# Weights laid out by unit, the router's rounding moved ahead, and an end in halves, in a two-model transformer kernel

## The chip, the core and the metric

The kernel runs on one core of a Trainium2 chip. The metric is the device time of one execution in microseconds (us); the time before is the median of three runs. Five engines work at once: TensorE (PE, matrix products, with PEld for the loads of its stationary operand), VectorE (DVE), ScalarE (ACT), GpSimd (POOL) and SyncE (SP). They meet by semaphores. DMA engines move data between the memory off the core and the on-chip memory of 128 partitions; products land in PSUM, eight banks of 512 fp32 numbers per partition.

## The reference

One sequence of 256 tokens, width 1024, goes through two models of two layers each, all in fp32. All weights are used once or, in the experts' stage, once per round.

```python
for l in range(2):                      # first model
    mod = silu(c) @ w_ada[l] + b_ada[l] # six vectors: shifts, scales, gates
    proj = modulate(rmsnorm(x, norm1_g[l]), shift1, scale1) @ w_in[l]
    # three attentions (latent, stick-breaking, block), gated, merged
    x = x + gate1 * (merged @ w_out[l])
    h = modulate(rmsnorm(x, norm2_g[l]), shift2, scale2)
    x = x + gate2 * (square(relu(h @ w_ff1[l])) @ w_ff2[l])
x = rmsnorm(x, final_norm_g)
x = layer_norm(a * x + retention(x), ...)        # second model, layer 0
x = layer_norm(a * x + swiglu(x, ffn_w_in, ffn_w_out), ...)
x = layer_norm(a * x + sparse_attention(x), ...) # layer 1
logits = x @ w_router                            # 8 experts, the best 2 per token
gate = softmax over the best 2
x = layer_norm(a * x + sum_e gate_e * swiglu(x, moe_w_in[e], moe_w_out[e]), ...)
```

## The kernel before

**Products.** An fp32 product is made of three products of rounded parts: `hi*whi + lo*whi + hi*wlo`. Weights come in units of 512 KB, [128 partitions, 2 blocks, 512 columns]. For each unit SP issues one load into a ring of buffers (`raw`, 4 deep; 12 deep in the experts' stage, over `raw`, `mod_b`, `work` and `spare`), ACT rounds it into `whi` (L1386), DVE subtracts into `wlo` (L1969), and PE runs the products: `unit` (L466 with whi, L472 with wlo) or, where the next stage wants tile 0 early, `by_tile` with `half_unit` (L486, L491). `pass_units(n)` is the place in the programs of ACT and DVE where n units are split, three units ahead of PE (`LEAD`). Activations are turned (transposed) on PE against an identity (L519, L566, L577) and split into `xh`, `xl` or `yh`, `yl` by ACT and DVE (L1440, L1447, L2052, L2059).

**Loads.** The weights lie in memory as the reference has them. `rows` (L3221) picks 256 rows and 512 columns as [p, 2, 512], so each partition gets two runs of 2 KB. SP issues them in the order of use, in loops for the dense SwiGLU and the experts. `load` (L3168) waits until the buffer's former unit has been split. Modulation weights (`w_ada`) go through the one buffer `ada_raw` or, in between, through `raw`; DVE sums them by L1990 and L1993, and `mod_used` lets SP load the next.

**Start.** 16 units of `w_ada` are loaded into idle buffers (`first_raw`, L3324), with x (1 MB) after the eighth; PE and DVE sum them, DVE scales and shifts x, and the first projection follows.

**From the sparse stage to the experts.** The last chunk of the sparse stage runs by tile (`last_chunk`, L1226). DVE's `layer_norm_by_tile` (L2560) adds the columns (L2538), takes moments (L2542), asks ACT for the root (L1532) and scales (L2554, L2557); it turns tile 0 and splits units in between. Then `experts` starts: PE turns both tiles of x (`turn_tiles`, L558), waits for one more hand-over from DVE (L1232), and runs the router's 24 products (L1238). That hand-over comes after ACT has rounded the router (L1861), DVE has taken its remainder (L2922), ACT has rounded x into `xth` (L1863) and DVE has made `xtl` (L2926). The logits are turned, DVE finds the best two (L2932 to L2950), ACT takes the exponential (L1867), PE counts places (L1250 to L1254), DVE forms the gates and the number of rounds, scales x by ALPHA (L2971), and all engines read the number of rounds. SP holds back all expert loads but the first three until then.

**Experts' loop.** For each of eight experts the tokens that chose it are gathered by products with a one-hot matrix (L1266), 128 at most in a round. An expert has seven steps; each step has eight units of the way in (`step_in`), the turn of the hidden part, and four of the way out (`step_out`). At an expert's end ACT rounds the output (L1875, 128 x 1024), DVE takes the remainder (L2993), PE scatters it by the one-hot's transpose (L1285, L1286) in four pieces, and DVE adds them to x (L3003). These pieces are woven into the next expert's units. The loop over experts runs two experts a pass.

**End.** After the last expert there is no next unit to hide these steps. DVE takes the moments of both tiles (L2515), ACT both roots (L1923), DVE scales tile by tile (L2527, L2530), and one store of 1 MB (L3350) writes x.

## Time and profile before

| What | us |
|---|---|
| Median of three runs | 2870.45 (2865.42 to 2870.57) |
| Profiled execution, its time | 2874.83 |
| Profiled execution, its span | 2872.9 |
| PE busy | 2683.1 |
| DVE busy | 2114.7 |
| ACT busy | 1610.5 |
| Mean granted clock of PE | 0.962 of full speed |
| Data moved | 666.09 MB |

A view of the profile is read as follows. A row of a timeline has start, duration, engine, line of the kernel, operation, what is written from what, and in brackets the idle time of the engine before it and who ended that. A row of the waits has the engine and line that waited, the one that released it, and the total, the number and the longest. The chain is followed back from the last instruction, at each step to what released it. PEclk is the clock granted to PE: 1.00 is 2.4 GHz, 0.50 is 1.2 GHz. Durations of PE's products overlap, so their pace is read from the chain or from starts.

### The profile page before, as it was taken

The numbers are of one execution on the slowest core, as the hardware profiler recorded it, in microseconds if no ns is written. First come the engines' busy times: TensorE is split into PE (matmuls) and PEld (weight loads), VectorE is DVE, ScalarE is ACT, GpSimd is POOL, SyncE is SP. The second block draws the span as 40 slices with busy tenths as digits, with TensorE's granted clock in tenths as the row PEclk, the third lists the DMA queues.
The fourth block names the chain that finished last, engine by engine and source line by source line (L and its number), as shares of the span: only waits on it lengthen the run. The fifth ranks groups of instructions, "written<-read, shape, count | busy, mean of one in ns | idle before, by whom it ended". The sixth has DMA issues, their size and how long they took to land.

```text
span 2872.9 us, 39552 instructions
## 1 busy us (share of the span) xinstructions
PE 2683.1 (93%) x12874; PEld 2166.5 (75%) x12874; DVE 2114.7 (74%) x2488; ACT 1610.5 (56%) x2094; POOL 21.5 (1%) x39
## 2 busy tenths in 40 slices
PE   7899999988999999999999887899999999999997
PEld 5677778876777787777997765688878878888875
DVE  6765577677556755866556855699989988999998
ACT  3544444445544444444444543577767777777775
POOL 0000000000000000000000000000000000000000
PEclk8999999999999999999999978899999999999998
DMA  8655468755545655645655411799989999999995
GB/s 300 196 156 166 154 199 266 242 183 170 169 147 164 204 188 155 219 150 153 194 181 166 137 44 44 262 353 329 365 300 364 330 342 334 345 347 331 366 358 199
DMA packets 358114, 666.09 MB, mean 232 GB/s; under 512 B 23024, under 2 KB 57456, under 8 KB 357344
## 3 DMA queue, kind: packets, MB, share of 16 engines
q1 hardware_dynamic: 354080, 647.66, 67.3%
q0 software_dynamic: 3904, 16.76, 1.8%
q8 instruction: 73, 1.20, 0.2%
q14 instruction: 57, 0.47, 0.0%
HBM read 663.29 MB, written 1.05 MB: 231 GB/s over the span
## 4 chain that ended last, share of the span: by engine, by line
PE 81%; DVE 8%; ACT 4%; issue 2%; DVEq 2%; DMA 1%; SPq 0%; ACTq 0%
PE ps L466 44%; PE ps L472 22%; PE ps L486 2%; DVE wlo L1969 2%; PE ps L577 2%; ACT whi L1386 1%; PE ps L491 1%; PE ps L1266 1%; PE ps L676 1%; DVE mod_sum L1993 1%; DMA ada_raw<-in_w_ada 1%; PE ps L788 1%; DMA proj<-in_w_ada 1%; PE ps L646 0%; ACT att L1608 0%
## 5 line engine op out<-in xcount | busy, mean ns | idle before, releaser
L1969 DVE TENSOR_TENSOR wlo<-raw,whi 128x1024 fp32r<-128x1024 f32 x709 | 863.4, 1224 | 452.9 <-ACT whi L1386 441.1
L1386 ACT ACTIVATE whi<-raw 128x1024 fp32r<-128x1024 f32 x709 | 746.0, 1059 | 703.1 <-PE ps L472 615.1
L466 PE MATMUL ps<-whi,xh 128*128 128x512 f32 (+3 forms) x1248 | 457.3, 377 | 4.5 <-ACT proj L1426 4.0
L466 PE MATMUL ps<-whi,xl 128*128 128x512 f32 (+3 forms) x1248 | 443.5, 366 | 0.0
L466 PE MATMUL ps<-whi,gathered_hi 128*128 128x512 f32 x896 | 362.8, 405 | 9.7 <-ACT whi L1386 6.3
L466 PE MATMUL ps<-whi,gathered_lo 128*128 128x512 f32 x896 | 356.1, 397 | 0.0
L472 PE MATMUL ps<-wlo,xh 128*128 128x512 f32 (+3 forms) x1248 | 293.5, 362 | 0.0
L472 PE MATMUL ps<-wlo,gathered_hi 128*128 128x512 f32 x896 | 283.3, 397 | 0.2 <-DVE wlo L1969 0.2
L466 PEld LDWEIGHTS ps<-whi,xh 128*128 128x128 f32 x1248 | 240.4, 193 | 46.1 <-ACT proj L1426 4.8
L466 PEld LDWEIGHTS ps<-whi,xl 128*128 128x128 f32 x1248 | 240.5, 193 | 36.9 <-issue 2.2
L472 PEld LDWEIGHTS ps<-wlo,xh 128*128 128x128 f32 x1248 | 215.8, 191 | 38.4
L466 PE MATMUL ps<-whi,yh 128*128 128x512 f32 (+2 forms) x592 | 236.8, 402 | 4.4 <-DVE yl L2059 2.2
L466 PE MATMUL ps<-whi,yl 128*128 128x512 f32 (+2 forms) x592 | 229.1, 389 | 0.0
L1969 DVE TENSOR_TENSOR wlo<-spare,whi 128x1024 fp32r<-128x1024 f32 x168 | 204.5, 1224 | 19.0 <-ACT whi L1386 17.4
L1969 DVE TENSOR_TENSOR wlo<-mod_b,whi 128x1024 fp32r<-128x1024 f32 x168 | 205.5, 1223 | 17.7 <-ACT whi L1386 12.6
L1386 ACT ACTIVATE whi<-spare 128x1024 fp32r<-128x1024 f32 x168 | 179.0, 1065 | 52.0 <-PE ps L472 52.0
L1386 ACT ACTIVATE whi<-mod_b 128x1024 fp32r<-128x1024 f32 x168 | 178.3, 1061 | 52.5 <-PE ps L472 52.1
L466 PEld LDWEIGHTS ps<-whi,gathered_hi 128*128 128x128 f32 x896 | 169.6, 189 | 48.5 <-ACT whi L1386 7.2
L472 PEld LDWEIGHTS ps<-wlo,gathered_hi 128*128 128x128 f32 x896 | 169.3, 189 | 41.9 <-DVE wlo L1969 0.7
L466 PEld LDWEIGHTS ps<-whi,gathered_lo 128*128 128x128 f32 x896 | 169.8, 189 | 37.1
L466 PE MATMUL ps<-whi,hidden_hi 128*128 128x512 f32 x448 | 178.5, 398 | 2.3 <-DVE hidden_lo L2059 1.3
L466 PE MATMUL ps<-whi,hidden_lo 128*128 128x512 f32 x448 | 176.9, 395 | 0.0
(417 smaller groups left out, 3587.2 us busy)
## 6 DMA issues: line engine op xcount, KB each, us to landing
raw<-in_moe_w_in SPq DMA_DIRECT2D x227, 512.0 KB, 5.4
spare<-in_moe_w_in SPq DMA_DIRECT2D x165, 512.0 KB, 5.6
mod_b<-in_moe_w_out SPq DMA_DIRECT2D x165, 512.0 KB, 5.4
raw<-in_w_ff SPq DMA_DIRECT2D x128, 512.0 KB, 4.6
raw<-in_w_in SPq DMA_DIRECT2D x96, 512.0 KB, 3.7
work<-in_moe_w_in SPq DMA_DIRECT2D x56, 512.0 KB, 5.5
work<-in_moe_w_out SPq DMA_DIRECT2D x56, 512.0 KB, 5.2
ada_raw<-in_w_ada SPq DMA_DIRECT2D x48, 512.0 KB, 4.5
```

Source lines behind the costliest of these rows:

```text
L466: e.matmul(ps[0:lhs[2], banks[t], at:at + width], part[:, k0 + j, t * P:t * P + lhs[2]], whi[:, slot, w], start=first and j == 0 and part ...
L472: mm = e.matmul(ps[0:lhs[2], banks[t], at:at + width], lhs[0][:, k0 + j, t * P:t * P + lhs[2]], wlo[:, slot, w], start=False, stop=last an ...
L486: e.matmul(ps[:, bank, at:at + width], part[:, k0 + j, t * P:(t + 1) * P], whi[:, slot, w], start=first and j == 0 and part is lhs[0], sto ...
L491: mm = e.matmul(ps[:, bank, at:at + width], lhs[0][:, k0 + j, t * P:(t + 1) * P], wlo[:, slot, w], start=False, stop=last and j == blocks - 1)
L577: tr = e.transpose(ps[:, bank, (j * tiles + t) * P:(j * tiles + t + 1) * P], src(t, b + j), ident)
L676: mm = e.matmul(ps[:, 4 + t, h * HD:(h + 1) * HD], side_pT[g][:, at:at + P], v(b, h), start=b == 0, stop=b == t)
L788: mm = e.matmul(ps[:, 4 + t, (h0 + h) * HD:(h0 + h + 1) * HD], own_pT[i % 2][:, w], proj[:, b, at:at + HD], start=b == 0, stop=b == t)
L1266: mm = e.matmul(ps[:, bank, j * P:(j + 1) * P], part[:, t, k * P:(k + 1) * P], onehot[b][:, t, :], start=t == 0, stop=t == 1)
L1386: e.activation(whi[:, slot, :], src, ACT.Copy).then_inc(split_hi, 1)
L1969: e.tensor_tensor(wlo[:, slot, :], src, whi[:, slot, :].bitcast(F32), ALU.subtract).then_inc(split_lo, 1)
L1993: last = e.scalar_tensor_tensor(total, w[:, j, :], c_col[:, k:k + 1], total, ALU.mult, ALU.add)
```

## The change

Four parts, in one version.

1. **Layout.** Weights other than the narrow part of `w_in`, `w_uq`, the `cmp` weights and the gates of the sparse stage are rearranged before the launch (`in_tiles`), so that each unit of 512 KB lies in one piece, 4 KB for each partition; `tile` takes the place of `rows` in the loads. `ffn_w_in` is laid out in four blocks of 256 columns. The narrow part of `w_in` and the gates become arrays of their own. The number of loads and their order stay.
2. **Router.** The router is rounded at unit 30 and its remainder taken at unit 31 of the sparse stage. `layer_norm_ahead_of_experts` takes the place of `layer_norm_by_tile` there: no units are split in it, and tile 1's columns are added before tile 0 is turned. PE's router products no longer wait for `xth` and `xtl`. Three splits, `xtl` and the scaling by ALPHA stand at new places of DVE's program. PE runs 14, 4 and 8 products on zeros (`idle`) after the turn of tile 0, after the logits' turns and after the place products. ACT runs one small Exp and one small Silu ahead of their use.
3. **Rounding of an expert's output** in two halves of 512 columns on ACT and DVE; the scatter goes by halves first and then by tiles, and its bank goes by tile.
4. **End.** Moments and roots by tile; the last scaling and the store in pieces: tile 0 whole, tile 1 in two halves.

```diff
+IDLE = (14, 4, 8)
...
             def experts(e):
-                turn_tiles(e, lambda t, b: x[:, t, b * P:(b + 1) * P], KB)
+                def idle(n):
+                    for _ in range(n):
+                        e.matmul(ps[:, 5, :], zero[0:1, 0:P], zero[0:1, :], start=True, stop=True)
+                tile_turns(src, 0)(e)
+                idle(IDLE[0])
+                tile_turns(src, 1)(e)
                 turned(e)
                 clear(e)
-                source(e)
...
+                idle(IDLE[1])
                 source(e)
...
+                idle(IDLE[2])
                 source(e)
...
-                    return [part(t, n) for t in range(NT) for n in range(2)]
+                    return [part(t, n) for n in range(2) for t in range(NT)]
...
             def experts(e):
                 turn_second(e)
-                vec(e)
-                e.activation(router_h, router, ACT.Copy).then_inc(act_ready, 1)
-                vec(e)
                 e.activation(xth, x[:, :, :], ACT.Copy).then_inc(act_ready, 1)
+                e.activation(st[:, 30:31], k_("eps"), ACT.Exp)
...
-                    e.activation(eh, ps[:, 2:4, :].rearrange("p b n -> p (b n)"), ACT.Copy).then_inc(out_hi, 1)
+                    for n in range(2):
+                        e.activation(eh[:, n * 512:(n + 1) * 512], ps[:, 2 + n, :], ACT.Copy).then_inc(out_hi, 1)
...
                 def one_round(e, r):
+                    e.activation(st[:, 30:31], k_("eps"), ACT.Silu)
...
+            def layer_norm_ahead_of_experts(e, units, src):
+                pass_units(e, 1)
+                take_gain(e, 0)
+                take_gain(e, 1)
+                tile_done(e)
+                add_columns(e, 0, 1, src(0, 1))
+                tile_deviation(e, 0)
+                normed_tile(e, 0)
+                e.wait_ge(unit_used, c.at("unit", RING + units - 1))
+                add_columns(e, 1, 1, src(1, 1))
+                tile_deviation(e, 1)
+                turn_first(e)
+                normed_tile(e, 1)
...
             def experts(e):
+                pass_units(e, 1)
                 turn_second(e)
-                e.wait_ge(extra_small, 80)
-                to_act(e)
-                from_act(e)
-                e.tensor_tensor(router_l, router, router_h.bitcast(F32), ALU.subtract)
-                e.drain()
-                to_act(e)
+                pass_units(e, 1)
                 from_act(e)
                 e.tensor_tensor(xtl, x[:, :, :], xth.bitcast(F32), ALU.subtract)
-                to_pe(e)
+                e.drain()
+                e.tensor_scalar(x[:, :, :], x[:, :, :], ALPHA, None, ALU.mult)
...
                 to_act(e)
+                pass_units(e, 1)
                 from_act(e)
...
-                e.tensor_scalar(x[:, :, :], x[:, :, :], ALPHA, None, ALU.mult)
...
+            def tile(w, column, group, groups=4):
+                return w[bass.ds((column * groups + group) * P, P), :]
...
+            rows_out = out.rearrange("o (t p) n -> p (o t) n", p=P)
             sp.wait_ge(x_done, 1)
-            sp.dma_start(out.rearrange("o (t p) n -> p (o t) n", p=P), x[:, :, :]).then_inc(stored, 16)
-            sp.wait_ge(stored, 16)
+            sp.dma_start(rows_out[:, 0, :], x[:, 0, :]).then_inc(stored, 16)
+            for h in range(2):
+                sp.wait_ge(x_done, 2 + h)
+                sp.dma_start(rows_out[:, 1, h * 512:(h + 1) * 512], x[:, 1, h * 512:(h + 1) * 512]).then_inc(stored, 16)
+            sp.wait_ge(stored, 48)
...
+def in_tiles(w, blocks=UROWS):
+    *lead, rows, columns = w.shape
+    wide = D // blocks
+    w = w.reshape(*lead, rows // (blocks * P), blocks, P, columns // wide, wide)
+    k = len(lead)
+    w = w.transpose(*range(k), k + 3, k, k + 2, k + 1, k + 4)
+    return w.reshape(*lead, -1, D)
```

## Rows read from the trace of the kernel before

**Rows 1.** The page: busy time by engine, PE first, share of the span, instructions

```profile
PE 2683.1 (93%) x12874; PEld 2166.5 (75%) x12874; DVE 2114.7 (74%) x2488; ACT 1610.5 (56%) x2094; POOL 21.5 (1%) x39
```

**Rows 2.** Windows: PE, PEld, DVE, ACT, POOL busy; PEclk; DMA share; GB/s

```profile
46.00:1765.00 1719.00, 1598.91 (x8095) 1306.32 (x8095) 1118.56 (x1419) 799.40 (x1183) 14.69 (x24) 0.96 0.55 172
...
1870.00:2840.00 970.00, 962.50 (x4313) 773.41 (x4312) 873.63 (x882) 740.00 (x825) 0.00 (x0) 0.99 0.97 344
```

**Rows 3.** Waits, 1870 to 2840 us: total, times, longest

```profile
ACT whi L1386 <- PE ps L472: 161.3, 418, 1.2
...
PE ps L466 <- ACT whi L1386: 6.3, 2, 3.8
```

**Rows 4.** Waits of the load queue (SP), 1870 to 2840 us

```profile
SPq L3218 <- DVE wlo L1969: 510.3, 627, 7.8
```

**Rows 5.** Windows of the start, columns as in rows 2

```profile
5.00:10.00 5.00, 2.75 (x4) 1.23 (x5) 3.67 (x18) 0.28 (x1) 0.00 (x0) 1.00 1.03 363
15.00:20.00 5.00, 1.98 (x4) 0.68 (x4) 0.89 (x2) 0.00 (x0) 0.00 (x0) 1.00 1.01 411
```

**Rows 6.** Chain that ended last, 0 to 46 us: start, us, what

```profile
9.19 16.30 DMA proj<-in_w_ada
```

**Rows 7.** The same chain, 46 to 120 us

```profile
56.10 4.68 DMA ada_raw<-in_w_ada
```

**Rows 8.** The same chain, 1776 to 1832 us

```profile
1776.05 0.46 PE ps L491 x2
...
1778.90 0.59 DVE x L2538
...
1780.95 1.23 DVE wlo L1969
...
1784.89 1.98 PE ps L566 x8
...
1790.87 2.29 DVE yl L2926
1793.45 4.29 PE ps L1238 x24
...
1809.71 7.07 PE ps L1266 x32
...
1818.67 2.07 PE ps L466 x4
...
1824.00 0.93 PE ps L466 x4
```

**Rows 9.** Timeline of DVE, 1798 to 1809 us; in brackets idle time before

```profile
1798.48 0.17 DVE L2074 COPY att<-ps 128x8 f32<-128x8 f32 x1 [5.31 <-PE ps L1245]
...
1805.64 1.20 DVE L2971 TENSOR_SCALAR x<-x 128x2048 f32<-128x2048 f32 x1
```

**Rows 10.** Timeline of ACT, 1832 us

```profile
1832.12 1.28 ACT L1627 ACT_TABLE_LOAD   x1
```

**Rows 11.** Window of the first gather, columns as in rows 2

```profile
1809.70:1818.60 8.90, 7.76 (x34) 7.19 (x34) 1.71 (x4) 1.83 (x4) 0.00 (x0) 0.50 1.02 387
```

**Rows 12.** Timeline of DVE at the end

```profile
2852.66 1.23 DVE L2993 TENSOR_TENSOR out_lo<-ps,out_hi 128x1024 fp32r<-128x1024 f32 x1
...
2859.09 2.65 DVE L2515 BATCH_NORM_STATS2 st<-x 128x6 f32<-128x512 f32 x4 [0.30 <-issue]
...
2866.99 1.28 DVE L2530 SCALAR_TENSOR_TENSOR x<-x,st,gain_b 128x1024 f32<-128x1024 f32 x1
```

**Rows 13.** Waits, 2090 to 2100 us

```profile
ACT out_hi L1875 <- issue: 6.3, 1, 6.3
...
PE ps L466 <- ACT whi L1386: 3.8, 1, 3.8
```

**Rows 14.** DMA issues of the whole run: xcount, KB each, us to landing

```profile
raw<-in_w_uq SPq DMA_DIRECT2D x6, 256.0 KB, 2.7
...
out<-x SPq DMA_DIRECT2D x1, 1024.0 KB, 3.9
```

More of the change, by code:

```diff
@@ L1279, in piece @@
                         def piece(e):
[L1280 removed]
+                            if t == 0:
                                 c.add("out")
@@ L1817, in sigmoids, with router_rounded @@
                     return e.activation(nsa_gate[:, 1, :], ps[:, b + 1, 0:48], ACT.Sigmoid)
+                def router_rounded(e):
+                    e.wait_ge(extra_small, 80)
+                    e.activation(router_h, router, ACT.Copy).then_inc(act_ready, 1)
                 at(4, twice_values)
@@ L1921, in act_program @@
             experts(act)
-            act.wait_ge(vec_ready_last, 1)
-            act.activation(st[:, 8:10], st[:, 0:2], ACT.Sqrt).then_inc(last_root, 1)
+            for t in range(NT):
+                act.wait_ge(vec_ready_last, t + 1)
+                act.activation(st[:, 8 + t:9 + t], st[:, t:t + 1], ACT.Sqrt).then_inc(last_root, 1)
         def gather_pieces(jobs, copies):
@@ L2990, in output @@
                 def output(e):
[L2991 to L2994 removed]
+                    for n in range(2):
+                        w = slice(n * 512, (n + 1) * 512)
+                        c.add("out")
+                        e.wait_ge(out_hi, c.at("out"))
+                        e.tensor_tensor(el[:, w], ps[:, 2 + n, :], eh[:, w].bitcast(F32), ALU.subtract).then_inc(out_lo, 1)
                 def add_output(b):
@@ L3196, in ada_rows @@
                 l, _, _, first = MOD_CHUNKS[m // 4]
-                return rows(a["w_ada"][l], m % 4 * UROWS * P)[:, :, first:first + 512]
+                return tile(a["w_ada"][l], first // 512, m % 4)
             def load_own_modulation(e, m):
@@ L3223, in rows, with columns, tiled @@
                 return w[bass.ds(at, blocks * P), :].rearrange("(j p) n -> p j n", p=P)
-            def columns(e, w, n_rows, first, width=UCOLS):
+            def tile(w, column, group, groups=4):
+                return w[bass.ds((column * groups + group) * P, P), :]
+            def columns(e, w, n_rows, first, width):
                 for i in range(units_of(n_rows)):
                     load(e, rows(w, i * UROWS * P)[:, :, bass.ds(first, width)])
-            def mlp_in(e, w_in, width, kind, s, units=range(8), first=False):
-                wide = kind[0]
+            def tiled(e, w, n_rows, column):
+                for i in range(units_of(n_rows)):
+                    load(e, tile(w, column, i, units_of(n_rows)))
@@ L3232, in mlp_in @@
+            def mlp_in(e, w_in, steps, kind, s, units=range(8), first=False):
                 for u in units:
                     if kind is SWIGLU and u < 4:
-                        load(e, rows(w_in, u % 2 * 512, 4)[:, :, bass.ds(s * wide + u // 2 * width, wide)])
+                        load(e, tile(w_in, s + u // 2 * steps, u % 2, 2))
                     elif kind is EXPERT:
-                        load_expert(e, rows(w_in, u % 4 * 256)[:, :, bass.ds(s * wide + u // 4 * width, wide)], first)
+                        load_expert(e, tile(w_in, s + u // 4 * steps, u % 4), first)
@@ L3237, in mlp_in, with mlp_out @@
                     elif u < 4:
-                        load(e, rows(w_in, u % 4 * 256)[:, :, bass.ds(s * wide + u // 4 * width, wide)])
-            def mlp_out(e, w_out, kind, s, by_columns=False):
-                order = [(kg, n) for kg in range(kind[0] // 256) for n in range(2)]
+                        load(e, tile(w_in, s, u % 4))
+            def mlp_out(e, w_out, steps, kind, s, by_columns=False):
+                groups = kind[0] // 256
+                order = [(kg, n) for kg in range(groups) for n in range(2)]
@@ L3285, in layer @@
                             for k in range(2):
-                                load(e, rows(a["w_out"][l], (2 * half + k) * UROWS * P)[:, :, n * 512:(n + 1) * 512])
+                                load(e, tile(a["w_out"][l], n, 2 * half + k))
             def experts(e):
```

169 lines of the change are left out of this document (84 added, 85 removed).

## The prediction

> **What bounds the kernel now.** I read the page first: TensorE (PE) is busy 93% of the span, and the chain that ended last is mostly PE [rows 1]. Then the stages. The experts' stage, 1870 to 2840 us, is a third of the span: PE is busy 962.5 of 970 us, while the DMA engines are busy 0.97 of it at 344 GB/s [rows 2]. Two resources look full, so the waits have to say which is late. ScalarE (ACT), which rounds each weight unit, waits for PE 418 times (161.3 us), and no wait for a DMA is in that list; PE waits for ACT twice [rows 3]. The load queue itself waits for VectorE (DVE) to free a buffer, 627 times, 510.3 us [rows 4]. So loads run ahead of need and the stage is PE's. Its pace in the chain is 0.93 us for four products with whi and 0.46 us for two with wlo, 1.40 us a unit [rows 8].
>
> That leaves the places where PE stands still or runs at 1.2 GHz: the start, where loads are late [rows 5, 6]; the modulation loads of the two attention layers [rows 7]; the way from the sparse stage's last layer norm to the first expert unit, 1776 to 1824 us [rows 8 to 11]; two stops inside the experts' loop [rows 13]; and the end [rows 12].
>
> **The change part by part.** The sum is against the profiled execution: 2874.83 us (span 2872.9), which lies 4.4 us above the 2870.45 us median. I carry differences over to the median.
>
> *Layout of the weights.* Each unit's 512 KB becomes 4 KB a partition in one run instead of two of 2 KB. The number of loads, their order and waits are unchanged; only their speed can change. In the experts' stage a faster load brings nothing: the queue waits for buffers anyway. If that cover were gone, PE would wait for units. At the start loads are on the path: the load of proj ends 16.30 us after its issue [rows 6], and DVE's first sums hang on it at 25.5 us. The rate was 363 GB/s in 5 to 10 us and 411 in 15 to 20 us, when x (rows of 4 KB) was among the loads [rows 5]. So 4 KB runs are worth between 0 and 13%. I take 5%, nearer to the low end since x was only a part of that traffic and the engines were full in both rows: over about 20 saturated us that is 0.9 us (0 to 2). From 25.5 to 42 us the start hangs on DVE, which is untouched.
> The trace reaches 411 GB/s from HBM with one core busy. The Trainium skill ("DMA: Bandwidth & Descriptors", Where 436 GB/s comes from) says the HBM side binds at about 358 GB/s; by it 4 KB runs would bring nothing here, 2853.3 us in all. The row speaks against that cap. The same page (Why small descriptors are slow) gives some 3 cycles a packet beside 32 bytes a cycle; my estimate from it is 134 against 131 cycles for 4 KB, 2%, or 0.4 us.
> The modulation's chunks that use ada_raw have one buffer: load, two DVE sums, next load. Four of these loads are in the chain, 4.5 to 6.8 us each; one stands for them [rows 7]. 5% of some 21 us, less where a fixed latency stays, is 0.8 us (0 to 1.6).
>
> *Layer norm before the experts.* Before, DVE turned tile 0 (two subtractions of about 0.69) before it added tile 1's columns at 1778.9, and it put a wlo split of 1.23 us (1780.95) ahead of tile 1's scaling [rows 8]. PE had ended the products at 1776.5, so the add can start at 1776.6. The chain from there to tile 1's turn was 6.0 us; it loses the split (1.2) and gains the two subtractions (1.3) in the shadow of ACT's root. The turn moves from 1784.89 to 1782.7: **2.2 us**.
> *Router.* Between the turn (1784.89) and the router's products (1793.45) lie 8.56 us [rows 8]: the turn, router_hi on ACT, router_lo on DVE, then xth on ACT and xtl on DVE (2.29), since the products waited for all of it. The rounding moves to units 30 and 31 of the sparse stage (ACT 0.26 us and DVE 0.22 us there; from 46 to 1765 us ACT is busy 799 and DVE 1119 of 1719 us [rows 2], so I cost it at nothing; without that cover it would cost those 0.5 us). The products then need only the turn's parts: 3.3 us after the turn's start, at 1785.5 to 1786.0. xtl, one split (1.23) and the ALPHA scaling (1.20) now run on DVE beside the products: 1785.3 + 1.2 + 2.3 + 1.2 with a wait for xth gives 1790.3. The products (4.29 us at mixed clock) end at 1788.4 to 1790.3, so DVE's copy of the logits, 1798.48 before [rows 9], goes to 1790.3. What is late next is this scaling on DVE, not PE. **8.2 us** so far, the first 2.2 included.
> *After it.* The scaling (1.20 at 1805.64) no longer stands before the rounds' value [rows 9]; a short wait for ACT's copy (0.4) falls away. The split placed after the exponential's hand-over delays DVE by 1.2 us, but the place products on PE (about 3.2 us) end later than DVE's chain then does. Together **9.7 us** by the first gather (1809.71 before). Reading the value stays. SP's remaining first loads start with it, 9.7 us earlier, as before.
>
> *Idle products.* 14, 4 and 8 products on zeros stand in PE's gaps. At 2.4 GHz they take about 0.23 us each (3.3, 0.9, 1.9 us), and the gaps are 5.3, 3.8 and 2.5 us, so they cost nothing; at 1.2 GHz the last 8 take 3.7 us and would put the gather 0.3 to 1 us later. What they can bring: before, the gather was PE-busy 7.76 us at a granted clock of 0.50 [rows 11], which is 1.2 GHz, after a gap of 6.6 us (1786.87 to 1793.45) and shorter ones; it took 7.07 us, and the two units after it 5.33 us (1818.67 to 1824.00) for 2.8 warm [rows 8]. At 2.4 GHz the gather is 3.5 us: 6.0 us at most. The trace before has no idle products in a gap, so 0 and 6 are the ends. A granted clock of 0.99 on average held through PE's short waits in the experts' stage [rows 2], which lies on the side of 6; gaps of 1.6 to 2.9 us remain around the idle products, which lies on the side of 0. I take **4 us**.
> The Trainium skill ("TensorE: Matmul & The Clock Gate", Part 1) has a clock that is released by activity, and Part 4 says that turns in PE mode do not count as such; the idle products are ordinary ones, so by it they would count and the turns between them not. No row here shows either.
> *Silu's table.* 1.28 us of table load stood between PE's last product of the first chunk and the activation [rows 10]. Loaded ahead, the activation starts when PE ends (1832.4 for 1833.41): **1.0 us**.
> *Rounding in halves.* Inside the loop ACT and DVE each do 0.2 us more per expert, under PE. The scatter's new order of banks leaves the same number of products.
>
> *End.* The first half's remainder is ready 0.95 us sooner (half of DVE's 1.23 [rows 12] and of ACT's rounding, which is a little shorter, less some 0.2 for the fixed part of an instruction), and DVE's adds shift by that. Then the statistics by tile cost 4.0 us for 3.8 (2859.09 to the first scaling) [rows 12], the reciprocals and four halves for two whole passes 0.5 more: DVE ends 0.2 us sooner. The last store is 256 KB, not 1 MB: landing 3.9 us for 1 MB, 2.7 for 256 KB [rows 14], which is 1.2, and 1.9 by rate. Sum **1.7 us** (1 to 3).
>
> Sum: 0.9 + 0.8 + 9.7 + 4.0 + 1.0 + 1.7 = **18.1 us**. 2874.8 becomes 2856.7, and the median 2870.45 becomes **2852.4 us**.
>
> **Rivals.**
> (A) The clock is not held: PE turns tile 1 and runs the router's products cold (1.0 us more on the way), and the idle products give nothing. For it: PE fell cold in every gap of this stretch, and gaps remain. 18.1 - 4 - 1 = 13 us, **2857**.
> (B) The experts' stops change. Twice PE stood 3.8 and 2.5 us while ACT had nothing it waited for but "issue", at the loop's way back [rows 13]; with the cold clock after it about 5 us each. They fall together with full DMA queues, so shorter loads may shorten them, and a longer loop body may add one. Both gone: 18 + 10, **2842**. One more: 2857.
> (C) Slower: the new layout lowers the rate. A unit of 512 KB per 1.40 us is 374 GB/s at PE's pace, and the stage had 344 GB/s at a DMA share of 0.97 [rows 2], so there is no reserve. The price begins where the rate of contiguous units falls below 344: at 330 GB/s the stage's 334 MB take 1011 us for 970, **2893**. Against it: the highest rates of the trace came with 4 KB rows.
> (D) The gain does not reach the path: another wait (the exponential, the place products, SP's first units) takes the gather's place, and the stage ends within 5 us of before, **2867**.
>
> **How the numbers follow.** Forecast 0.55, A 0.24, B 0.08, C 0.06, D 0.07. The range from 2841 (B, or clock 6, start 2, end 3) to 2863 (A with none of the load terms, a shorter end gain and one longer stop) leaves out C, D and the tails. A measurement of this kernel tells about 0.2%, 5.7 us, from no change: C is slower; most of D is the same. Faster 0.88, same 0.06, slower 0.06.
>
> **What would show it.** Router products starting about 8 us after the last product of the sparse stage (17 before); a gather of 3.5 us at a granted clock of 1.00 if the idle products work, 7 us at 0.50 if A; DVE idle before its logit copy gone; no table load before the first Silu; in 5 to 35 us the same DMA share with some 5% more GB/s; the experts' stage at 344 GB/s still with no DMA in ACT's waits; the last store landing in some 2.5 us. The prediction is wrong if ACT starts to wait for units, or if the stops at the loop's way back multiply.

## The result and the profile after

Five runs of the changed kernel have a median of **2853.98 us** (2852.68 to 2857.76), five of the kernel before one of 2870.57 us. The ratio is **0.9949**, 95% interval 0.9938 to 0.9961: 0.5% faster, 16.6 us between the medians. The forecast was 2852.4 us, so the total came out as forecast, and in part by luck: two of its parts did not, and they cancelled. The profiled execution of the kernel after took 2853.45 us, that of before 2874.83, so the two traces differ by more than the medians: 21.2 us of span. The page of the kernel after, answering to [rows 1]:

```profile
span 2851.7 us, 39687 instructions
...
PE 2683.9 (94%) x12900; PEld 2165.7 (76%) x12900; DVE 2114.5 (74%) x2501; ACT 1609.8 (56%) x2105; POOL 21.5 (1%) x39
...
PEclk9999999999999999999999978899999999999999
```

Nothing of the work is gone: PE is busy 2683.9 us for 2683.1 (26 products on zeros are new). What went is time in which it stood still or ran at 1.2 GHz. The windows of the kernel after (columns as in [rows 2]), for the start [rows 5], the experts' stage [rows 2] and the first gather [rows 11]:

```profile
5.00:10.00 5.00, 3.58 (x5) 1.55 (x6) 3.76 (x17) 0.28 (x1) 0.00 (x0) 1.00 1.02 409
...
15.00:20.00 5.00, 2.66 (x6) 0.68 (x4) 1.50 (x2) 0.00 (x0) 0.00 (x0) 1.00 1.00 416
1855.00:2825.00 970.00, 965.29 (x4340) 775.00 (x4339) 879.85 (x894) 744.45 (x836) 0.00 (x0) 1.00 0.94 344
1799.30:1807.50 8.20, 7.75 (x35) 7.21 (x34) 1.68 (x3) 1.19 (x2) 0.00 (x0) 0.50 0.98 381
```

The start moves 409 GB/s where it moved 363, at the same DMA share. The experts' stage still has 344 GB/s. The gather is at a granted clock of 0.50, as before: the idle products ahead of it did not lift it.

**Where 21.2 us went.** I cut both spans at three instructions that both traces have: the first turn of tile 0 after the sparse stage, the first product of the first expert unit, and the start of the last rounding of an expert's output.

| Stretch | Before | After | Saved |
|---|---|---|---|
| start to the turn of tile 0 | 1776.35 | 1773.67 | 2.7 |
| turn of tile 0 to the first expert unit | 42.32 | 34.62 | 7.7 |
| first expert unit to the last rounding of an output | 1032.93 | 1025.05 | 7.9 |
| last rounding to the end | 21.3 | 18.4 | 2.9 |

The second stretch, in the chain that ended last of the kernel after, answers to [rows 8]:

```profile
1780.01 1.98 PE ps L520 x8
...
1783.44 4.74 PE ps L1235 x24
...
1794.99 3.52 PE ps L1224 x8
1798.52 0.85 PE ps L888 x2
1799.37 7.03 PE ps L1265 x32
...
1808.29 2.07 PE ps L467 x4
```

Turn of tile 1, router products, the last eight idle products (3.52 us at 1.2 GHz), the clearing of the expert banks, the gather (7.03 us) and the first unit, cold again. The third stretch holds an item that I had not put into the forecast. The waits at the first way back of the experts' loop, answering to [rows 13]:

```profile
ACT out_hi L1878 <- PE ps L473: 3.2, 1, 3.2
...
PE ps L467 <- ACT whi L1385: 0.8, 1, 0.8
```

ACT stood 3.2 us for 6.3, and PE 0.8 for 3.8; at the second way back PE stood 1.4 us for 2.5. From the 510th rounding of a unit, ahead of both stops, to the last it is 979.0 us for 985.2: with the cold clock behind them the two stops cost 6.2 us less. Of the 7.9 us of the stretch some 0.8 are Silu's table (below) and 0.9 are not traced to anything. The end, answering to [rows 12]:

```profile
2833.34 1.08 ACT L1878 ACTIVATE out_hi<-ps 128x512 fp32r<-128x512 f32 x2 [0.34 <-PE ps L473]
2834.17 1.28 DVE L3016 TENSOR_TENSOR out_lo<-ps,out_hi 128x512 fp32r<-128x512 f32 x2
...
2839.31 1.29 DVE L2514 BATCH_NORM_STATS2 st<-x 128x6 f32<-128x512 f32 x2 [0.30 <-issue]
...
2847.58 1.62 DVE L2531 SCALAR_TENSOR_TENSOR x<-x,st,gain_b 128x512 f32<-128x512 f32 x2
2848.39 1.20 SPq L3382 DMA_DIRECT2D out<-x  x2
```

### The profile page after: what moved, and what is told of

Same layout as the page of the kernel before. It is cut to its first block, busy times and chain, and to the rows that moved or that the text cites. A ratio compares the mean times of both kernels' runs of the same rounds, so it can differ in the third digit from the quotient of the medians.

```text
span 2851.7 us, 39687 instructions
## 1 busy us (share of the span) xinstructions
PE 2683.9 (94%) x12900; PEld 2165.7 (76%) x12900; DVE 2114.5 (74%) x2501; ACT 1609.8 (56%) x2105; POOL 21.5 (1%) x39
## 4 chain that ended last, share of the span: by engine, by line
PE 81%; DVE 8%; ACT 5%; issue 2%; DVEq 2%; DMA 1%; SPq 0%; ACTq 0%
PE ps L467 44%; PE ps L473 22%; PE ps L487 2%; DVE wlo L1974 2%; PE ps L566 2%; ACT whi L1385 2%; PE ps L492 1%; PE ps L1265 1%; DMA ada_raw<-in_w_ada 1%; PE ps L665 1%; DVE mod_sum L1998 1%; PE ps L777 1%; DMA proj<-in_w_ada 1%; PE ps L635 0%; ACT att L1607 0%
```

## Experiments

Twelve kernels, each run beside the kernel before on the same chip. The stretches are cut as above; "ACT idle" is ACT's idle time ahead of the rounding of an output at the first and second way back of the experts' loop. A stretch is of the one profiled execution of each kernel; the medians are of all its runs.

| Kernel | Median | Ratio (95%) | Turn of tile 0 at | To first unit | Experts' stage | End | ACT idle |
|---|---|---|---|---|---|---|---|
| before | 2870.57 | | 1776.4 | 42.3 | 1032.9 | 21.3 | 6.3, 5.0 |
| layout_alone | 2868.92 | 0.9995 (0.9986 to 1.0004) | 1774.0 | 42.4 | 1029.8 | 21.5 | 4.4, 4.5 |
| old_router | 2866.58 | 0.9994 (0.9982 to 1.0006) | 1770.9 | 42.4 | 1033.1 | 19.0 | 4.3, 3.5 |
| old_end | 2858.29 | 0.9963 (0.9950 to 0.9975) | 1774.1 | 34.4 | 1028.3 | 20.6 | 3.5, 3.6 |
| all_but_layout | 2854.83 | 0.9952 (0.9939 to 0.9966) | 1768.7 | 34.4 | 1027.7 | 18.3 | 3.6, 3.2 |
| after | 2853.98 | 0.9949 (0.9938 to 0.9961) | 1773.7 | 34.6 | 1025.1 | 18.4 | 3.2, 3.9 |
| no_silu | 2856.38 (one run) | | 1773.4 | 34.4 | 1028.5 | 18.3 | 3.6, 3.3 |
| no_idle | 2853.50 | 0.9945 (0.9930 to 0.9960) | 1771.5 | 33.9 | 1026.1 | 18.3 | 3.6, 4.2 |
| idle_full | 2850.39 | 0.9940 (0.9925 to 0.9955) | 1767.9 | 32.9 | 1025.4 | 18.3 | 2.9, 4.0 |
| idle_more | 2850.00 | 0.9933 (0.9917 to 0.9950) | 1775.8 | 31.9 | 1028.3 | 18.4 | 3.4, 3.9 |
| idle_close | 2851.29 | 0.9932 (0.9918 to 0.9945) | 1774.8 | 29.4 | 1030.6 | 18.4 | 4.5, 4.0 |
| pad_before | 2860.70 (one run) | | 1773.9 | 42.3 | 1021.5 | 21.1 | 0.3, 0.3 |
| pad_after | 2851.83 (one run) | | 1774.8 | 34.4 | 1022.5 | 18.4 | 0.3, 0.3 |
| close_and_pad | 2849.86 | 0.9930 (0.9916 to 0.9943) | 1767.5 | 29.7 | 1025.1 | 18.3 | 0.3, 0.3 |

### The layout alone, and all but the layout

```diff
-                load(e, rows(w, i * UROWS * P)[:, :, bass.ds(first, width)])
+                load(e, tile(w, column, i, units_of(n_rows)))
```

The first kernel is that of before with every load of this kind changed and nothing else; the second is the changed kernel with the loads of before.

> The kernel before with the new layout of the weights alone. Theory A (the layout pays only where loads are on the path): first rounding of a projection unit 1.5 to 2 us earlier (35.05 us before), the modulation loads some 0.3 us shorter each, the experts' loop as before with its two stops (PE idle 3.8 and 2.5 us at the loop's way back), about 2868 us, ratio 0.999. Theory B (the two stops of the experts' loop come from full DMA queues, and runs of 4 KB shorten them as in the changed kernel, where they are 0.8 and 1.4 us): 6 us more, about 2862 us, ratio 0.997, and the gain stays away in the kernel that has all the rest without the layout.

> The changed kernel with the weights laid out as before. Theory A: about 2 us slower than the changed kernel, 2856 us, ratio 0.995; the stops of the experts' loop are as short as in the changed kernel (0.8 and 1.4 us of PE idle). Theory B: the stops are back at 3 to 4 and 2.5 us, 2862 us, ratio 0.997. By both, the share of the DMA engines' time in 5 to 20 us is the same 1.0 and the rate 363 to 411 GB/s for 409 to 419.

The layout alone gave 0.9995 (0.9986 to 1.0004), and taking it out of the changed kernel 0.9952 for 0.9949. By the medians it is worth about 1 us, less than these measurements can tell from nothing. The windows of 5 to 10 and 15 to 20 us, of the layout alone and then of all but the layout (columns as in [rows 2]):

```profile
5.00:10.00 5.00, 3.66 (x5) 1.59 (x6) 3.70 (x17) 0.28 (x1) 0.00 (x0) 1.00 1.03 407
...
15.00:20.00 5.00, 2.57 (x6) 0.67 (x4) 1.50 (x2) 0.00 (x0) 0.00 (x0) 1.00 1.01 422
```

```profile
5.00:10.00 5.00, 2.88 (x4) 1.37 (x5) 3.67 (x18) 0.28 (x1) 0.00 (x0) 1.00 1.03 372
...
15.00:20.00 5.00, 1.98 (x4) 0.68 (x4) 1.17 (x3) 0.00 (x0) 0.00 (x0) 1.00 1.01 415
```

At a DMA share of 1.03 the rate is 407 GB/s with runs of 4 KB and 372 with runs of 2 KB; later, when rows of x (4 KB in both) are among the loads, 422 and 415. So the layout does what it says. In layout_alone it moves ACT's first rounding of a projection unit from 35.05 us to 33.07, and the four modulation loads of [rows 7] from 21.5 us to 20.1. In the experts' stage faster loads change nothing: the rate is 344 GB/s before and after.

For the stops, theory A's reading held for the second kernel: with runs of 2 KB they are as short as with 4 KB (PE idle 1.2 and 0.8 us). In the first they were shorter than before, but not as short (2.0 and 2.0 us of PE idle for 3.8 and 2.5, and 3.1 us less for the stage), which neither theory had said: ACT's and PE's programs are the same there, so the length of a stop also hangs on something else than their code. On what, no run isolates.

### The idle products: none, then 128 rows of data

```diff
-IDLE = (14, 4, 8)
+IDLE = (0, 0, 0)
```

> The changed kernel without its 26 products on zeros. Theory A (a product of one row of zeros does not hold the clock: it fell to 0.50 at 1777 us while 14 of them ran, and the gather after the last 8 ran at 0.50): turn of tile 1 1.97 us, gather at 0.50 and some 7 us as with them, the gather up to 1 us earlier because the last 8 took 3.6 us, total within 2 us of the changed kernel, 2852 to 2855. Theory B (they hold part of the clock): the way from the last turn of tile 0 to the first expert unit, 34.6 us in the changed kernel, becomes 2 to 4 us longer.

```diff
-                        e.matmul(ps[:, 5, :], zero[0:1, 0:P], zero[0:1, :], start=True, stop=True)
+                        e.matmul(ps[:, 5, :].rearrange("p (h k) -> p h k", h=4), ident16[:, :],
+                                 masks16[:, 0:P].rearrange("p (o k) -> p o k", o=1).broadcast_to([P, 4, P]),
+                                 start=True, stop=True)
```

> The changed kernel with its 26 idle products on 128 rows of data that are not zero (identity by masks, bf16, 512 columns) in place of one row of zeros: same count, same columns. Theory A (what counts is how much of the array works): the turn of tile 1 at 1.0 us in place of 1.97, the router products at 1.00 of the clock (2.5 us in place of 4.5), the 8 last ones 1.9 us in place of 3.6, the gather 3.5 us in place of 7: 4 to 8 us less in that stretch. Theory B (any gap of 1.5 us ends the clock, whatever ran before it): nothing changes, within 1 us.

Without idle products the stretch is 33.9 us, with them 34.6 and in four more kernels that have them 34.4. So the 26 products on one row of zeros cost 0.5 to 0.8 us and give nothing, as theory A of no_idle has it; the medians (2853.50, 2853.98) cannot tell them apart. The window of the gather in the kernel without idle products (columns as in [rows 2]):

```profile
1796.40:1803.40 7.00, 6.98 (x33) 7.00 (x33) 1.40 (x3) 0.60 (x1) 0.00 (x0) 0.50 0.94 360
```

With 14, 4 and 8 products on 128 rows, the first 14 and the turn of tile 1 in the timeline of PE:

```profile
1768.79 3.19 PE L1224 MATMUL ps<-masks,ident 128*128 128x512 bf16 x14
1774.26 1.97 PE L520 MATMUL ps<-const,x 128*128 128x128 f32 x8 [2.28 <-DVEq L2092]
```

and its gather in the windows:

```profile
1791.80:1798.90 7.10, 7.08 (x33) 7.01 (x33) 1.43 (x3) 0.60 (x1) 0.00 (x0) 0.50 0.99 379
```

All 14 ran at 2.4 GHz (3.19 us, 0.23 each). Behind them PE stood 2.28 us, and the turn of tile 1 was cold (1.97 us for 8 turns, 1.03 when warm). So was the gather. The stretch got 1.0 us shorter than with none, not the 4 to 8 that I had expected.

In the changed kernel's own trace the 14 on zeros took 3.70 us and the clock fell among them, which looks like a difference of the products. Other traces do not bear it out: in those of old_end, no_silu and pad_after the same 14 on zeros took 3.19 us as well, and the clock fell only behind them, 6.4 us after the start of the turn of tile 0, as it did with the full ones (6.3). The line of pad_after, and the window of the kernel before in which PE ran nothing at all:

```profile
1775.75 3.19 PE L1224 MATMUL ps<-zero 1*128 1x512 bf16 x14
```

```profile
1777.40:1784.80 7.40, 0.00 (x0) 0.00 (x0) 6.71 (x10) 0.88 (x3) 0.00 (x0) 0.86 0.00 0
```

A mean of 0.86 means 1.00 for the first 5.3 us of a complete standstill and 0.50 after it. So when the clock falls first is no measure of what ran just before. The kinds differ in one place only: behind the router's products the clock stayed up until 20.0 us after the turn of tile 0 with full products, and until 16.6 to 17.2 us with zeros (five kernels) or with none (16.7). That is one trace of the full kind, so theory A, that the kind of product counts, is not shown. Theory B is: the gaps left ended the clock with either kind.

### Closing the gaps

```diff
-IDLE = (14, 4, 8)
+IDLE = (24, 6, 3, 11, 14, 3)
...
+                idle(IDLE[1])        # after the turn of tile 1
+                idle(IDLE[2])        # after the router's products
-                idle(IDLE[1])
+                idle(IDLE[3])        # after the logits' turns
-                idle(IDLE[2])
+                idle(IDLE[4])        # after the place products
+                    idle(IDLE[5])    # ahead of the gather
```

> The changed kernel with 61 idle products (24 after the turn of tile 0, 6 after that of tile 1, 3 after the router's products, 11 after the logits' turns, 14 after the place products, 3 ahead of the gather) on 128 rows of data that are not zero, which leave no gap of PE over some 0.5 us. Theory A (it is the gaps left that end the clock; it fell at 1774.2 us in the run with 26 such products, right behind a gap of 2.28 us): turn of tile 1 in 1.0 us, router products in some 3 us in place of 4.5, gather at 1.00 in 3.5 us in place of 7.1; from the turn of tile 0 to the first expert unit 26 to 28 us (32.9 with 26 full ones, 34.6 in the changed kernel), total 2844 to 2847. Theory B (these products do not count either, or come too late): the gather stays at 0.50, and the queue of 61 products costs 0 to 3 us more, total 2850 to 2854.

The timeline of PE, with the turn of tile 1, the first place products and the idle products behind them:

```profile
1782.12 1.09 PE L520 MATMUL ps<-const,x 128*128 128x128 f32 x8
...
1792.23 0.39 PE L1252 MATMUL ps<-att,const 128*128 128x8 f32 x2 [1.10 <-DVEq L2977]
...
1794.26 6.73 PE L1224 MATMUL ps<-masks,ident 128*128 128x512 bf16 x17
```

The window in which those run:

```profile
1795.00:1800.00 5.00, 5.00 (x13) 1.81 (x12) 1.57 (x9) 1.49 (x2) 0.00 (x0) 0.50 0.48 153
```

The turn of tile 1 is warm (1.09 us). One gap is left, 1.10 us ahead of the place products, and behind it the clock is at 0.50 from 1793.3 until 1800.1: the last idle products took 0.44 us each for 0.22 and held up the gather, which started 26.1 us after the turn of tile 0 for 23.9. It was itself warm, and the first unit came at 31.9 us, where theory A had 26 to 28, and its total of 2844 to 2847 was missed too (2850.0). Closing that gap:

```diff
-IDLE = (24, 6, 3, 11, 14, 3)
+IDLE = (24, 6, 3, 15, 16, 4)
```

> As the run with 61 idle products of 128 rows, but 24, 6, 3, 15, 16 and 4 of them: the one gap left there, 1.10 us behind the 11 products after the logits' turns, is closed, since behind it the clock fell at 1793.3 us and 14 products took some 5 us, so that the gather started at 26.1 us after the turn of tile 0 in place of 23.9. Theory A (the clock holds while ordinary products of 128 rows leave no gap of about a microsecond): 1.00 from the turn of tile 0 through the gather, the gather at 24.5 to 25 us, the first expert unit at 29 to 30 us (31.9 there, 34.6 in the changed kernel), total 2847 to 2850. Theory B (the clock falls somewhere in that stretch whatever PE does): one stretch at 0.50 in it again, first unit at 31 us or later, total 2850 to 2854.

The window from the turn of tile 0 to the first unit, and the gather and the first unit in the chain that ended last:

```profile
1774.80:1804.00 29.20, 27.49 (x165) 16.27 (x163) 20.42 (x50) 9.83 (x18) 1.06 (x2) 1.00 0.35 121
```

```profile
1798.78 3.64 PE ps L1269 x32
...
1804.16 1.29 PE ps L467 x4
```

The granted clock is 1.00 from the turn of tile 0 through the gather, which takes 3.64 us for 7.03, and the first unit comes at 29.4 us, 5.2 earlier than in the changed kernel and 4.5 earlier than without idle products. It fell again 1.0 us into the first unit, for 3.4 us. Theory A held for the stretch, and the 4 us that the forecast put on the clock were there to be had, but not with 26 products in these gaps. Zeros in all six places were not run, so whether it takes full products is open. The median (2851.29, ratio 0.9932) is 2.7 us below the changed kernel's, about half of it, and the intervals overlap. This kernel's experts' stage was longer, and here it was PE itself that stood, at both ways back (4.2 and 2.6 us). The first, and the queue q8 in the page of this kernel:

```profile
PE ps L467 <- issue: 4.2, 1, 4.2
```

```profile
q8 instruction: 91, 1.49, 0.2%
```

All kernels with 61 idle products or fewer have 73 packets on q8. What these queues carry is taken up with the stops, below.

### The router part and the end, each as before

The changed kernel with `layer_norm_by_tile`, `turn_tiles`, the router's rounding and remainder behind the turns, and the splits and the ALPHA scaling at their old places:

> The changed kernel with the router, the layer norm ahead of the experts, the scaling by ALPHA and the order of the splits as before (and no idle products, no early Exp). Theory A (this part is worth what the stretch shows): from the turn of tile 0 to the first expert unit 42.3 us again (34.6 in the changed kernel), 7.7 us, and the turn of tile 0 where the changed kernel has it, total about 2862; stops of the experts' loop as short as in the changed kernel (0.8 to 1.4 us), as the rounding in halves is in it. Theory B (the stops hang on where the code of ACT lies, which this part shifts): a stop of 2 us or more is back in the loop, total 2864 to 2868.

The changed kernel with the rounding whole, the scatter by tiles first, moments, roots and scalings as before, and one store:

> The changed kernel with the rounding of an expert's output, the scatter's order, the last moments, roots, scalings and the store as before. Theory A (the end alone): from the last product of the last unit to the end 2.9 us longer, stops of the loop as in the changed kernel, total about 2857. Theory B (the halves of the rounding also shorten the stops at the loop's way back): the stops are back at 2 to 4 us of PE idle as in the kernel before, 4 to 6 us more, total 2861 to 2863.

Without the router part all the rest gives 0.9994 (0.9982 to 1.0006), nothing that can be measured; the change is mostly the router part, 12.6 us of the 16.6 by the medians. The stretch explains 7.7 of these. The other large difference of the traces is in the experts' stage, 1033.1 us for 1025.1, though none of this part's code runs there. Its stop at the first way back, in ACT's instructions by line (columns: busy and mean, then the idle time before them and who ended it), and in DVE's timeline:

```profile
L1876 ACT ACTIVATE out_hi<-ps 128x512 fp32r<-128x512 f32 x2 | 1.1, 594 | 4.3 <-issue 4.3
```

```profile
2090.36 1.29 DVE L2993 TENSOR_TENSOR out_lo<-ps,out_hi 128x512 fp32r<-128x512 f32 x2 [5.71 <-issue]
```

ACT stood 4.3 us and then DVE 5.7, both on nothing but "issue". So theory B held here (also by the median, 2866.58), and the halves of the rounding, which this kernel has, are not what shortens the stops.

With the old end the part behind the last rounding took 20.6 us in that run for 18.3, 2.3 more, and the median is 4.3 us above the changed kernel's; the stops stayed short (3.5 and 3.6 us on ACT). Theory A, at a little less than the 2.9 us of the two main traces.

### The table ahead of the first chunk

```diff
-                    e.activation(st[:, 30:31], k_("eps"), ACT.Silu)
```

> The changed kernel without the small Silu ahead of the gather, so that the table is loaded at the first chunk of the experts. Theory A: a table load of 1.28 us stands between PE's last product of the first chunk and the activation, PE idle there 2.6 us as in the kernel before, not 1.8. Theory B: ACT has the time for it elsewhere, idle stays 1.8 us. The three first roundings of a unit start up to 1.3 us earlier without it if ACT was late there.

The timeline, with the table load and PE's first product behind the activation:

```profile
1821.72 1.28 ACT L1626 ACT_TABLE_LOAD   x1
...
1824.61 0.79 PE L467 MATMUL ps<-whi,gathered_hi 128*128 128x512 f32 x1 [2.60 <-DVE att L2247]
```

In the changed kernel the same product waits 1.83 us, and 2.61 in the kernel before: 0.8 us, as by theory A. (The median of this kernel is that of one run.) The first roundings of a unit are no earlier without it.

### Moving ACT's code

Sixty more instructions on ACT, none with work, once, where ACT is idle:

```diff
             def experts(e):
+                for _ in range(120):
+                    e.wait_ge(const_ready, 16)
                 turn_second(e)
```

(Two of these waits make one instruction.)

> The kernel before with 120 waits that are long fulfilled (60 more instructions, no work) on ACT at the start of its experts' part, where it is idle; only the place of the code of the experts' loop moves, on ACT alone. Theory A (the two stops are ACT's reload of its code at the loop's way back, and where the code lies sets how early it begins): the first reload begins within 1 us of the start of ACT's last rounding of a unit, as in all kernels with the new router part, where it came 2 to 3.8 us after it in the kernel before; or the stops grow; PE idle changes from 3.8 and 2.5 us by over 1 us. Theory B (the stops come from full DMA queues or from the work around them): 3.8 and 2.5 us stay within 0.7.

> The changed kernel with the same 60 more instructions on ACT at the same place. Theory A (place of the code): the stops of 0.8 and 1.4 us change by over 1 us, so that the 984 to 978 us by which the experts' stage got shorter is shown to be chance of the code's place. Theory B: they stay at 0.8 to 1.5 us as in seven other kernels with the new router part, and that part itself, not the place of ACT's code, is their cause.

The rounding of an output at the first way back, ACT by lines, in the kernel before, then in it with the 60 instructions:

```profile
L1875 ACT ACTIVATE out_hi<-ps 128x1024 fp32r<-128x1024 f32 x1 | 1.0, 1023 | 6.3 <-issue 6.3
```

```profile
L1877 ACT ACTIVATE out_hi<-ps 128x1024 fp32r<-128x1024 f32 x1 | 1.0, 1026 | 0.3 <-PE ps L472 0.3
```

The DMA queues show what ACT stood for. In 2077 to 2097 us of the kernel before, then in 2080 to 2350 us of the kernel after:

```profile
q8 instruction: 1, 0.02, 0.3%
q14 instruction: 2, 0.02, 0.2%
```

```profile
q14 instruction: 7, 0.06, 0.1%
```

The queue q14 carries instructions, in pieces of 8 KB (57 packets, 0.47 MB in the whole run), and q8 in pieces of 16 KB (73 packets, 1.20 MB). That q14 serves ACT and q8 PE is read from what changes with which program, not from a label. In the kernel before, two pieces on q14 come after ACT's last rounding of a unit and before the next instruction starts (2092.3 and 2094.1 us; ACT resumes at 2095.9). In pad_before the same view of 2080 to 2350 us has the loads' queue alone:

```profile
## 3 DMA queue, kind: packets, MB, share of 16 engines
q1 hardware_dynamic: 48510, 93.51, 97.6%
```

In the kernel after the two pieces come at 2077.2 and 2079.0 us and ACT resumes at 2080.8, though the view of the waits puts that wait down to PE. In both padded kernels the queue q14 has no packet in these 270 us, ACT stands 0.3 us, PE does not stop, and the stage takes 1021.5 us for 1032.9 (pad_before) and 1022.5 for 1025.1 (pad_after). The one run of pad_before, 2860.7 us, is below all nine of the kernel before beside it (2865.9 to 2871.6). Theory A of pad_before held in its core, that the place of ACT's code alone sets the stops, but neither of its two outcomes was this one: the reload did not begin earlier, it was gone. Theory A of pad_after held: the two stops of PE, 0.8 and 1.4 us, went.

### Both together

> The run with idle products that leave no gap (24, 6, 3, 15, 16 and 4 of them, 128 rows) and the 60 more instructions on ACT ahead of its experts' part, together. Theory A (the two gains are of different places and add): from the turn of tile 0 to the first expert unit 29.4 us at a clock of 1.00 as there, the experts' stage 972.4 us between the 510th and the last rounding as in the two padded kernels (983.2 in the run with close idle products alone, 977.9 in the changed kernel), no reload of code of 8 KB between 2080 and 2590 us; total 2851.3 less 10.8, about 2841, ratio 0.990. Theory B (the place of code is set by more than ACT's: PE has 35 more instructions here): stops are back, 2846 to 2852.

The code queue in 2061 to 2075 us, and PE's stop in its timeline:

```profile
q8 instruction: 3, 0.05, 1.8%
```

```profile
2069.52 0.49 PE L467 MATMUL ps<-whi,gathered_hi 128*128 128x512 f32 x1 [2.60 <-ACT whi L1390]
```

ACT's stops are gone (0.3 us) and the stretch is 29.7 us. But PE has a stop of 2.6 us at the first way back, with three pieces of 16 KB on queue q8 around it; none is left at the second. This kernel has the PE program of idle_close, and yet 82 packets on q8 for 91 there: whether PE's loop is reloaded does not hang on PE's own program alone. The median is 2849.86 us, ratio 0.9930 (0.9916 to 0.9943). That lies below the changed kernel's 0.9949, though the intervals overlap, and it is not the 2841 of theory A but within the 2846 to 2852 of theory B; the profiled run (2842.5 us) is the fastest of five and not typical. That the stop on PE is a reload of PE's code fits the packets (73 on q8 in the other kernels), but was not tested by moving that code alone.

## Why the forecast came out, step by step

**The bound.** Right. PE stays the bound of the experts' stage, the load queue's cover holds, and a layout that loads faster brings nothing there.

**Start and modulation loads**, 0.9 and 0.8 us. Right in kind, a little small: the rate rose by 9% (372 to 407 GB/s) in 5 to 10 us and by 2% in 15 to 20 us, where I took 5% throughout; in layout_alone the first rounding of a unit came 2.0 us earlier (35.05 to 33.07), and the four modulation loads took 1.4 less. The rows also spoke against the two readings of the Trainium skill ("DMA: Bandwidth & Descriptors"): against its cap of about 358 GB/s from HBM (Where 436 GB/s comes from) stand 407 to 422 GB/s, and against my estimate of 2% from its cost of a small descriptor (Why small descriptors are slow) 9% in the first window.

**Layer norm**, 2.2 us. Right to the tenth: the turn of tile 1 came 6.34 us after that of tile 0 for 8.54.

**Router**, 8.2 us at the copy of the logits. 6.9 came (7.1 in no_idle). The start of the products was right (9.8 us after the turn of tile 0 for 17.1), but they took 4.74 us, all but the last 0.8 at 1.2 GHz, so PE's products and not DVE's scaling were late next. The term that was mis-sized is their clock: I had them end at 1788.4 to 1790.3 on the old time axis; they ended at 1790.9. The 1788.4 did not even follow from my own 4.29 us, which gives 1789.8 at the earliest.

**After it**, 1.5 us more to the gather. Without idle products it is 1.4 (the gather starts 24.9 us after the turn of tile 0 for 33.4, 8.5 saved in all, for 9.7 forecast); with them the gather starts at 25.6 us, 0.75 later, with the last eight at 1.2 GHz ahead of it, inside the 0.3 to 1 that the prediction gave for that case.

**Idle products**, 4 us. **Wrong.** Their effect was the end of the bounds, 0, less that 0.75. The step that failed is the choice between the ends: I took the granted clock in the experts' stage, where PE's short waits lie among full products, as the nearest row, and the gaps of 1.6 to 2.9 us that remain as the lesser reason. The runs showed that the gaps decide. With the same 14, 4 and 8 as full products on 128 rows the stretch was 1.0 us shorter than with none; with full products in every gap (idle_close) the granted clock was 1.00 through the gather and the stretch 4.5 us shorter. Whether one row of zeros would have done in every gap is open. The Trainium skill ("TensorE: Matmul & The Clock Gate", Part 1 and Part 4) has the clock follow activity and PE-mode turns not count; by it I had the idle products count as ordinary ones. The two traces without gaps fit it: the clock stayed at 1.00 across the 8 turns between full products. Whether products on one row of zeros count, no run here shows. Rival A, the clock not held, is what happened here; its total of 2857 was missed because of the stops.

**Silu's table**, 1.0 us. 0.8 came.

**End**, 1.7 us. 2.9 came. Up to the last add 1.5 us were saved, where I had 0.95: in the trace after, the scatter ran warm, in that of before it went cold in the middle (granted clock 0.50 in 2855 to 2857 us). Statistics and scalings cost 0.7 more, as forecast. From the last scaling to the end it was 2.5 us for 4.6, 2.1 less, nearer to the 1.9 by rate than to the 1.2 that I took.

**The experts' stops**, put at no change. **Wrong**, and it made up for the idle products: 6.2 us. Rival B had a price of 10 us for both gone and a chance of 0.08, with shorter loads as the mechanism. The mechanism was not that: all_but_layout has short stops with runs of 2 KB. (Nor had ACT "nothing it waited for but issue" at both stops, as the prediction reads them: the view of the second puts its 5.0 us down to PE.) Moving ACT's code by 60 instructions takes the stops away in both kernels, and with the router part undone (no padding) they are long again. So moving ACT's code is enough to take the stops away, in one trace of each kernel. That it is also what shortened them in this change fits the table (the stage takes 1025.1 to 1028.5 us in seven unpadded kernels with the new router part, 1029.8 to 1033.1 in the three without it, and again 1030.6 in idle_close, where only PE's program got longer and PE stood itself), but it was not isolated: the part cannot be had without moving code.

**What lies ahead of the change.** The turn of tile 0 came between 1767.5 and 1775.8 us in nine kernels whose programs are the same up to there (after, no_silu, no_idle, old_end, pad_after and the four with full idle products). Two rows show how. The same four turns behind the same wait of 2.42 us, in the kernel before and then in the kernel after:

```profile
732.12 1.06 PE L622 MATMUL ps<-const,work 128*96 128x128 f32 x4 [2.42 <-DVE kT L2074]
```

```profile
727.31 0.61 PE L611 MATMUL ps<-const,work 128*96 128x128 f32 x4 [2.42 <-DVE kT L2079]
```

In one the clock fell, in the other it did not. In the stretch of 1636 to 1776 us of the kernel before it was the other way round (the kernel after lost 5.9 us there that it had gained earlier). Such falls come and go by 1.3 us and more each without any cause in the program: for the same products PE was busy 1629 us up to that turn in close_and_pad and 1639 us in idle_more. It is the likely reason why runs of one kernel spread by 5 to 13 us and why the profiled executions differ by 21.2 us while the medians differ by 16.6; as only one run of each kernel has a trace, that is not shown. A sum made on one pair of profiles cannot be held to better than that.

So the total of 18.1 us came near the 16.6 by luck: by the sum of a chain term that nearly held (8.5 for 9.7), one that was absent (4, rather -0.75) and one that had not been counted (0, rather 6.2). With the pieces as measured on the profiles: 2.7 + 7.7 + 7.9 + 2.9 = 21.2. The ends of the range were not added up right either: without rival B its best terms give 18.1 + 2 + 1.1 + 1.3 = 22.5 us, or 2848 and not 2841, and rival A without the load terms, with the shorter end and one longer stop gives 2865 and not 2863.

## What to carry to other kernels

Work that a consumer waits for only because it was written ahead of it (here xl of x, a split, a scaling) was the main gain here, and its size could be read from the chain to about 1 us (8.5 for 9.7). To hold PE's clock through a stretch of small steps, fill every gap and read the granted clock of the stretch afterwards; products on 128 rows did it here, lighter ones were not tried without gaps, and a filler that left one gap gave little. One trace is not enough to say what made the clock fall: compare several kernels that are alike up to there. Before a difference of under 1% is put down to an edit, look at the instruction queues and the engines' waits at loops' way back, and move the code by some instructions: here that alone was worth 10 us in one run, more than half of the change.

## What the runs showed of the hardware that I had not expected

**Code is reloaded in a loop, and whether it is hangs on its place.** ACT's loop over the experts had stops of 6.3 and 5.0 us at its two ways back, with two 8 KB pieces on queue q14 each, 1.8 to 2.1 us apart; 60 instructions ahead of the loop made it 0.3 and 0.3, and no piece was loaded in 270 us. The Trainium skill ("Advanced Engine Details and Errata", ISA Cache) has an instruction cache of 32 KB (128 KB on TensorE) with two lines of 16 KB; the pieces on q14 were of 8 KB, half of such a line, those on q8 of 16. How it decides what to reload, no run here shows.

**The moment at which the clock falls does not tell what ran just before.** The same 14 products on one row of zeros took 3.19 us at 2.4 GHz in three traces and 3.70 and 4.15 us, with the clock falling among them, in two; in the kernel before the clock stayed at 1.00 for 5.3 us in which PE ran nothing. Full products in every gap kept it at 1.00 for 29 us, in two traces (idle_close, close_and_pad).

**A gap of 1.10 us can be enough to lose the clock** (idle_more; closing it kept the clock), and one of 2.42 us need not be (kernel after, 727 us).

**One core read 407 to 422 GB/s from HBM** at a DMA share of 1.00 to 1.03 with runs of 4 KB, and 363 and 372 with runs of 2 KB at 1.03 (415 when rows of x were among them).
